# P scaled by GpSimd instead of VectorE in the attention loop, and VectorE's copy of P^T moved ahead of its part of the scaling

## The reference

```
def masked_softmax(s, mask):
    s = jnp.where(mask, s.astype(jnp.float32), NEG)
    m = jnp.max(s, axis=-1, keepdims=True)
    e = jnp.where(mask, jnp.exp(s - m), 0.0)
    return e / jnp.maximum(jnp.sum(e, axis=-1, keepdims=True), 1e-30)
...
        p = masked_softmax(sc, kpos[None, :] <= t[:, None])
        o = jnp.einsum('bhqk,bkhd->bqhd', p.astype(v.dtype), v)
```

## Time and profile before

| | |
|---|---|
| median of 3 runs | 2791.77 us (2791.64 to 2791.93) |
| profiled execution | 2792.11 us, of which the span from the first to the last instruction is 2790.3 us |
| PE busy | 2773.4 us, 99% |
| DVE busy | 1493.6 us, 54% |
| ACT busy | 1228.8 us, 44% |
| POOL busy | 14.8 us, 1% (28 instructions) |
| mean granted TensorE clock | 0.999 of full speed |
| DMA | 504.08 MB read, 181 GB/s over the span |

### The profile page before, as it was taken

The page is one execution under the profiler, slowest core; times in us unless marked ns, Lnnn a source line. Parts: engine busy times, 40 slices in busy tenths (PEclk is TensorE's granted clock), DMA queues, the critical chain, the costliest instruction groups (busy, mean ns, idle before and its releaser), DMA issues.

```text
span 2790.3 us, 30469 instructions
## 1 busy us (share of the span) xinstructions
PE 2773.4 (99%) x13217; PEld 2311.5 (83%) x13217; DVE 1493.6 (54%) x1205; ACT 1228.8 (44%) x1291; POOL 14.8 (1%) x28
## 2 busy tenths in 40 slices
PE   9999999999999999999999999999999999999999
PEld 7888778888888888888888888888888888888887
DVE  5455765455455445455455684665554454544555
ACT  5336663345554343343444545344434334333453
POOL 0000000000000000000000000000000000000000
PEclk9999999999999999999999999999999999999999
DMA  7644036655455565655556654545655555555555
GB/s 235 218 146 165 31 111 207 195 186 206 166 180 183 195 196 181 196 182 195 185 193 205 200 181 153 179 153 183 215 192 190 190 193 185 192 195 194 173 182 175
DMA packets 256437, 508.15 MB, mean 182 GB/s; under 512 B 8162, under 2 KB 18992, under 8 KB 255408
## 3 DMA queue, kind: packets, MB, share of 16 engines
q1 hardware_dynamic: 254112, 495.61, 54.2%
q0 software_dynamic: 2016, 10.36, 1.1%
q10 hardware_dynamic: 176, 0.23, 0.0%
HBM read 504.08 MB, written 2.10 MB: 181 GB/s over the span
## 4 chain that ended last, share of the span: by engine, by line
PE 86%; DVE 0%; ACT 0%; issue 0%
PE acc L679 27%; PE acc L678 27%; PE acc L683 27%; PE tb L664 2%; PE tb L1172 0%; PE acc L886 0%; PE acc L885 0%; PE acc L883 0%; PE tb L1162 0%; PE tb L1191 0%; PE acc L1080 0%; PE tb L1222 0%; PE tb L1202 0%; PE tb L1223 0%; PE tb L1047 0%; PE tb L1066 0%
## 5 line engine op out<-in xcount | busy, mean ns | idle before, releaser
L1826 DVE TENSOR_TENSOR wlo<-raw,whi 128x2048 fp32r<-128x2048 f32 (+1 forms) x465 | 1063.9, 2290 | 866.3 <-ACT whi L1346 865.7
L1346 ACT ACTIVATE whi<-raw 128x2048 fp32r<-128x2048 f32 (+1 forms) x465 | 889.5, 1914 | 980.9 <-PE acc L683 781.6
L678 PE MATMUL acc<-whi,ahi 128*128 128x512 f32 (+1 forms) x1968 | 767.8, 391 | 0.4 <-DVE alo L1918 0.4
L679 PE MATMUL acc<-whi,alo 128*128 128x512 f32 (+1 forms) x1968 | 762.6, 388 | 0.0
L678 PE MATMUL acc<-whi,bhi 128*128 128x512 f32 x1528 | 597.1, 391 | 0.0
L679 PE MATMUL acc<-whi,blo 128*128 128x512 f32 x1528 | 595.2, 390 | 0.0
L683 PE MATMUL acc<-wlo,ahi 128*128 128x512 f32 (+1 forms) x1968 | 484.3, 388 | 0.0
L678 PEld LDWEIGHTS acc<-whi,ahi 128*128 128x128 f32 x1968 | 370.4, 188 | 74.9 <-DVE wlo L1915 0.9
L679 PEld LDWEIGHTS acc<-whi,alo 128*128 128x128 f32 x1968 | 370.7, 188 | 73.8
L683 PEld LDWEIGHTS acc<-wlo,ahi 128*128 128x128 f32 x1968 | 367.3, 188 | 75.3
L683 PE MATMUL acc<-wlo,bhi 128*128 128x512 f32 x1528 | 377.9, 389 | 0.0
(11 more groups left out here) (334 smaller groups left out, 1557.9 us busy)
## 6 DMA issues: line engine op xcount, KB each, us to landing
raw<-in_w_ff SPq DMA_DIRECT2D x128, 1024.0 KB, 5.2
raw<-in_w_in SPq DMA_DIRECT2D x119, 1024.0 KB, 5.1
raw<-in_w_gate SPq DMA_DIRECT2D x44, 1024.0 KB, 5.2
raw<-in_w_up SPq DMA_DIRECT2D x44, 1024.0 KB, 5.1
raw<-in_w_down SPq DMA_DIRECT2D x44, 1024.0 KB, 5.1
raw<-in_w_out SPq DMA_DIRECT2D x16, 1024.0 KB, 5.1
raw<-in_w_o SPq DMA_DIRECT2D x16, 1024.0 KB, 5.1
raw<-in_w_ple_gate SPq DMA_DIRECT2D x16, 1024.0 KB, 5.3
```

What stands on the lines that cost most here:

```text
L678: nc.tensor.matmul(out_(t), hi[:, kt, tt(t)], whi[:, slot, wc(k)], start=first and k == 0, stop=False)
L679: nc.tensor.matmul(out_(t), lo[:, kt, tt(t)], whi[:, slot, wc(k)], start=False, stop=False)
L1346: nc.scalar.activation(whi[:, g % SPLIT, 0:n_], raw[:, g % RAW, 0:n_], ACT.Copy).then_inc(w_hi, 1)
L1826: V.tensor_tensor(wlo[:, g % SPLIT, 0:n_], raw[:, g % RAW, 0:n_], whi[:, g % SPLIT, 0:n_].bitcast(F32), ALU.subtract).then_inc(w_lo, 1)
```

## The change

DVE still forms the factor in `scale_of` (the reciprocal, and for NSA its product with the gate), but no longer multiplies P. It raises a new semaphore, `factor`. GpSimd waits for it, multiplies P in place by the factor over the same two shapes, and raises `scaled`, for which PE waits as before. The wait of DVE for `scaled` of the item before stays ahead of the reciprocal, since `rinv` has one buffer. And in DVE's step m the copy of P^T of m-2 stands ahead of the factor of m-1.

```
@@ gpsimd, between its loads of the compression weights and its load of h
+                for it in items:
+                    if it["kind"] == "attn":
+                        p = it["p"]
+                        r = rinv[:, 1 if it["fam"] == "nsa" else 0, :].rearrange("p (n t) -> p n t", t=TT)
+                        pool.wait_ge(factor, it["n"] + 1)
+                        for t in range(TT):
+                            x = prob[:, p % 2, :, t * P:(2 * t + 1) * P]
+                            last = nc.gpsimd.tensor_tensor(x, x, r[:, :, t:t + 1].to_broadcast([P, 2, (t + 1) * P]), ALU.mult)
+                        last.then_inc(scaled, 1)
@@ vector, scale_of
                 linked()
-                link(V.reciprocal(rinv[:, 0, :], sums[:, p % 4, :]))
-                linked()
+                ins = V.reciprocal(rinv[:, 0, :], sums[:, p % 4, :])
                 r = rinv[:, 0, :].rearrange("p (n t) -> p n t", t=TT)
                 if it["fam"] == "nsa":
+                    link(ins)
+                    linked()
                     if it["n"] == 0:
                         dve.wait_ge(gsig_ready, 1)
                     hd = 4 * it["g"] + 2 * it["pair"]
-                    link(V.tensor_tensor(rinv[:, 1, :].rearrange("p (n t) -> p n t", t=TT), r,
-                                         gsig[:, :, hd:hd + 2, it["br"]].rearrange("p t h -> p h t"), ALU.mult))
-                    linked()
-                    r = rinv[:, 1, :].rearrange("p (n t) -> p n t", t=TT)
-                for t in range(TT):
-                    x = prob[:, p % 2, :, t * P:(2 * t + 1) * P]
-                    last = V.tensor_tensor(x, x, r[:, :, t:t + 1].to_broadcast([P, 2, (t + 1) * P]), ALU.mult)
-                last.then_inc(scaled, 1)
+                    ins = V.tensor_tensor(rinv[:, 1, :].rearrange("p (n t) -> p n t", t=TT), r,
+                                          gsig[:, :, hd:hd + 2, it["br"]].rearrange("p t h -> p h t"), ALU.mult)
+                ins.then_inc(factor, 1)
@@ vector, attend
-                    for step, k in ((scale_of, m - 1), (middle_of, m - deep + 1)):
+                    for step, k in ((middle_of, m - deep + 1), (scale_of, m - 1)):
```

More of the change, by code:

```diff
@@ L376, in build @@
         pts_done, ptv_done = sem("pts_done"), sem("ptv_done")
-        scaled, o_hi, o_lo = sem("scaled"), sem("o_hi"), sem("o_lo")
+        scaled, o_hi, o_lo, factor = sem("scaled"), sem("o_hi"), sem("o_lo"), sem("factor")
         qk_var, qk_rstd, qk_ready, r_var, r_rstd, r_ready = map(sem, (
```

## The result

The changed kernel takes 2801.04 us (median of 7, 2799.99 to 2801.43) against 2791.77 (median of 7, 2791.58 to 2793.01): 9.3 us more. The ratio on record, taken over the runs and not from the two medians (which give 1.0033), is 1.0029 with an interval of 1.0020 to 1.0038. The profiled execution has a span of 2798.7 us, 8.4 more than before.

What follows compares the result with a forecast made beforehand. PE was taken as the bound, busy 99%, with waits in the attention loop set by latency. Turn-by-turn additions, GpSimd's chain bounding 19 turns, summed to 13.6 us, giving 2805.4 us, range 2795 to 2822.

Steps and rivals of the forecast that it cites:

- the clock: Rival that PE's longer waits lower its granted clock from 1.00 in the loop, costing tens of us; chance 0.03.
- the new tie between neighbours: Neighbouring items: scaling waits for the previous item's transposes and copy; turns 3.17 to 3.99 us, four times, +3.3.
- DVE's lost work: DVE loses 48 multiplications, 25 us of its time, worth only what waited behind them since DVE isn't the bound.
- c: Time from the end of DVE's factor to the start of PE's transposes: 0.15 + 1.9 + 0.15 = 2.20 us.
- The pair: GpSimd's two multiplications of one item, taken as 1.9 us, the middle between 1.03 and 2.83.
- the two hand-overs: Semaphores DVE to GpSimd and GpSimd to PE, where one stood before; taken as 0.15 us each.
- MLA: Turns of MLA items, 356.22 to 374.74 us: 5.39 each, four are 21.56 instead of 18.52, +3.0.
- NSA: Turn from an NSA item over a projection step to another: 5.08 to 5.59 us, three groups of four, +1.5.
- into the next group: Turn from a group's last item to the next's first: 4.70 to 5.59 us, +0.9 three times and 0.7, +3.4.
- The fourth group's pair of turns: Turn of 4.63 us grows by 1.0, but 0.7 of PE's idle time in the following stretch gives way: +0.3.
- the tail: Loop's last turns: 3.70 us grows by 0.3, the last of 2.86 becomes 3.79, +0.9; value products' 1.36 wait goes.
- Rival B: DVE's two-SBUF-operand work (compression steps 4 x 1.6, halves 3 x 1.22) and GpSimd exclude each other: 10 us, 2815; chance 0.22.

Runs made afterwards that it cites:

- e2_pool_old_order: The changed kernel with DVE's two steps back in their old order, factor ahead of the copy, GpSimd still scaling: 2794.5 us, +1.8 against before.
- e3_apart: The changed kernel with DVE's halves and remainders moved away from GpSimd's scaling, nothing left out: 2797.4 us, +4.7 against before.
- the useless product: The changed kernel plus one useless DVE product of two SBUF operands, 128x428, behind each of the 24 factors: 2806.8 us, +14.0 against before.
- the reduction: The changed kernel plus one useless DVE maximum over one SBUF operand, 128x428, behind each factor: 2800.9 us, +8.1 against before.

## Why the prediction was right, and where it wasn't

The place and the mechanism held. The loss is in the loop and isn't given back; the clock stayed; GpSimd's wait ahead of its load of `h` shows no cost; the new tie between neighbours exists and has the predicted form: 0.86 + 0.55 + 0.38 + c is 3.53 with the measured c, the turn is 3.50. DVE's lost work won next to nothing here: three turns with a compression step are as long as before (8.32, 6.80 and 6.80 us for 8.33, 6.84 and 6.85). In the old order, `e2_pool_old_order`, the same turns are 0.25 to 0.33 shorter.

**The term that was mis-sized is c**: 2.20 us in the sum, 1.74 measured. The pair was taken as 1.9 us, the middle between bounds far apart, and is 1.61 to 1.65; the two hand-overs were taken as 0.15 each and are 0.07 and 0.06. That they would be unlike 0.15 was one of the prediction's own signs of being wrong, and it came: they make 0.17 of the 0.46 missing, the pair 0.29. The measured c also lies at the very edge of the forecast's own bounds, 1.75 to 2.7. So by kind of turn, expected and measured: MLA 5.39 and 4.97; NSA 5.59 and 5.17; neighbours 3.99 and 3.50; into the next group 5.59 and 5.17. The fourth group's pair of turns, priced at +0.3, is 0.3 shorter (11.57 to 11.23). By the prediction's own rate, 19 x 0.46 = 8.7 us of the 13.6 weren't there, which leaves 4.9. The turns bear this out. Take the changed kernel's +8.4 us of span and put the two turns with a half at 3.5 us, as in `e3_apart` (-1.8), and the last two pairs at 1.61 instead of 2.42 (-1.6): 5.0 are left. So the walk by turns was sound. That `e3_apart` as a whole has +4.7 us is less of a proof, as it gains 1.1 in the first group and loses some of it in the tail, where a remainder now stands ahead of a copy.

**Rival B was true and was priced wrongly.** I gave it 0.22 and 10 us. By GpSimd's rows it costs 3.4 us: two pairs are 0.9 longer by a half and two 0.8 by the remainders. The 3.8 us between the stretches of the changed kernel and `e3_apart` (3.6 by the two medians, 4.6 by their distances from before, which was 1 us slower in the later comparison) hold 1.1 that isn't exclusion. The priced 6.4 us of the compression steps cost next to nothing, and the profile of the changed kernel says why. In all four groups DVE is the one that stands still there. In three nobody waits for it:

```profile
344.24 1.61 POOL L638 TENSOR_TENSOR prob<-prob,rinv 128x256 f32<-128x256 f32 x2 [3.56 <-DVE rinv L2121]
...
345.16 0.72 DVE L2096 TENSOR_TENSOR csum<-csum,gsig 128x8 f32<-128x8 f32 x1
```

In the first group the product at 280.56 us (L2088) takes 1.07 instead of 0.28, a half stands behind it, and ACT waits 2.07 us for the maxima where it waited 1.78: some 0.3 us, not separated by any run.

The time, 9.3 us, thus comes from two errors with opposite signs: 4.9 by the turns and 3.4 by the exclusion make 8.3, and the span grew by 8.4. That it lies as near to the forecast of 13.6 as it does is in part luck: a rival that the sum left out made up for a good third of what c took away. No row of before has GpSimd computing, so neither size could be read there. What could be read is that halves and remainders stand directly behind the factor in DVE's order; the tail was worked out without the remainders, which made its two turns +0.6 and +1.2 instead of +0.3 and +0.9.

The Trainium skill's rule on the shared port pair (SBUF, State Buffer, "SBUF: two separate sides") is borne out here for two SBUF operands, by 0.26 us beside the useless product and none beside the reduction, though the rows grow by less than the whole overlap. The Trainium skill's ratio of 1.96 between the engines (GPSIMD Engine Reference, "Performance versus the Vector engine") isn't what this shape shows: 1.61 us against 1.03 is 1.56.

What stays open: whether a longer DVE instruction with one SBUF and one PSUM operand leaves GpSimd alone too (the one beside it here takes 0.21 us), and why the loop starts up to 1.7 us earlier or later from one profile to another.

## What to carry to other kernels

An operation on an idle engine isn't free if its result is the next thing that the busy engine waits for: here it has 0.43 us of slack, and GpSimd's pair and hand-over take 0.7 more than DVE's. Measure the slack behind the operation first, in the timeline of one turn. Two changes that are harmless or good alone can be bad together: the moved copy gains 1.9 us with DVE's multiplication. With GpSimd's it costs 6.6 by the stretch, and 3.9 where the halves are kept apart, because it takes away the head start that the slower engine needs. Beside GpSimd keep DVE's work with two SBUF operands away, or let it fall where PE is the one that works. And test a new placing without the other engine too: 1.1 of the 3.8 us that it gained here came from DVE's own queue.

## What the runs showed of the hardware

- GpSimd multiplies 128x256 fp32 elements by a broadcast factor in 0.61 us and 128x512 in 1.04; DVE takes 0.42 and 0.69. The very first such instruction was as short as the others, 0.61 us.
- GpSimd starts 0.07 us after DVE's end and PE 0.06 after GpSimd's, hardly more than the 0.04 from PE to ACT. I had expected twice that.
- A copy by DVE from PSUM to SBUF, 128x384 fp32 in 0.56 us, lies wholly beside GpSimd's pair of 1.61 without making either longer (`e2_pool_old_order`). A sum of one PSUM and one SBUF operand takes 0.21 us beside the pair as it does elsewhere.
- The exclusion takes less than the overlap. Beside the useless product they overlap for 0.40 us and GpSimd's row grows by 0.27; beside DVE's multiplication 0.39 and 0.24; beside a half 1.06 (312.35 to 313.41) and 0.92. Perhaps GpSimd's instruction does without what is excluded for its first 0.13 to 0.15 us; no run separates that from a quick start after DVE's end. And it goes both ways: a DVE product of 8 elements, 0.17 us else, took 0.72, until 0.03 us after GpSimd's pair was through (345.88 and 345.85).
